# Two norms of a two-block transformer placed inside down projections, and queries and keys placed ahead of the other stream's

## The reference, cut to what matters

```python
def second_block(x, c, ctx, ...):
    for i in range(DEPTH):                       # 2 layers: pooling, attention
        a_l = modulate(rms_norm_2(h_lat, norm_g[i, 0]), sh1, sc1)
        a_c = modulate(rms_norm_2(h_ctx, norm_g[i, 0]), csh1, csc1)
        # layer 0: y = pool_mix(a, pool_w, pool_scale), for each stream
        # layer 1: y_l = attn_mix(a_c, a_l, ...): queries of a_l, keys and values of both
        h_lat = h_lat + g1 * y_l
        m_l = modulate(rms_norm_2(h_lat, norm_g[i, 1]), sh2, sc2)
        h_lat = h_lat + g2 * sq_relu_mlp(m_l, mlp_w1[i], mlp_w2[i])
        # layer 0: the same for h_ctx
    return rms_norm_2(h_lat, final_g)

def pool_mix(h, w, scale):      # p: window means of 2, 4, 8, 16 rows, less the row itself
    return einsum("blgc,gcd->blgd", p, w) * scale
```

## Time and profile before

| | us |
|---|---|
| median of 3 runs | 1587.86 (1587.66 to 1589.6) |
| the profiled execution | 1588.41 |
| its span, first to last instruction | 1585.9 |
| busy: PE, DVE, ACT | 1490.0, 1113.0, 760.0 |
| mean granted clock | 0.979 |

### The profile page before, as it was taken

How to read it: one execution, slowest core, us unless ns; L and a number is a source line. 1 busy time by engine, 2 the same in 40 slices (tenths; PEclk the granted TensorE clock), 3 DMA queues, 4 the chain that set the end, 5 groups by cost and what they waited for, 6 DMA issues and landing times.

```text
span 1585.9 us, 21196 instructions
## 1 busy us (share of the span) xinstructions
PE 1490.0 (94%) x8517; PEld 1202.0 (76%) x8517; DVE 1113.0 (70%) x1682; ACT 760.0 (48%) x1184; POOL 0.2 (0%) x4
## 2 busy tenths in 40 slices
PE   5999899999999799999999999899999998899997
PEld 3767778888787568888778878688787776778786
DVE  3566758998769868998676555867767685465656
ACT  3334544444544445344465544555545534455543
POOL 0000000000000000000000000000000000000000
PEclk9999999999999899999999999899999999999999
DMA  9993158888565757776647555486674740245452
GB/s 361 343 320 136 54 186 292 293 286 304 206 239 183 243 186 260 266 245 239 213 151 274 186 186 186 161 302 233 248 255 146 269 140 27 79 133 178 172 189 86
DMA packets 167913, 335.22 MB, mean 211 GB/s; under 512 B 8192, under 2 KB 109192, under 8 KB 167816
## 3 DMA queue, kind: packets, MB, share of 16 engines
q1 hardware_dynamic: 140992, 235.09, 43.8%
q10 hardware_dynamic: 26824, 98.79, 16.8%
HBM read 332.81 MB, written 1.05 MB: 211 GB/s over the span
## 4 chain that ended last, share of the span: by engine, by line
PE 59%; DVE 25%; ACT 8%; DMA 4%; issue 4%; ACTq 0%; SPq 0%; DVEq 0%
PE ps L1860 11%; PE ps L1861 11%; PE ps L1862 11%; PE ps L1929 11%; DVE wlo L1138 9%; PE ps L1930 5%; ACT whi L659 4%; DVE hbuf L1160 3%; DMA ring<-in_ada_w_dram 3%; ACT hbuf L679 2%; PE ps L1791 1%; DVE res L1226 1%; DVE work L1224 1%; PE ps L2024 1%; PE ps L2101 1%
## 5 line engine op out<-in xcount | busy, mean ns | idle before, releaser
L1138 DVE TENSOR_TENSOR wlo<-wraw,whi 128x1024 fp32r<-128x1024 f32 (+1 forms) x420 | 493.2, 1216 | 202.9 <-ACT whi L659 202.3
L659 ACT ACTIVATE whi<-wraw 128x1024 fp32r<-128x1024 f32 (+1 forms) x420 | 418.3, 1044 | 227.0 <-PE ps L1862 139.1
L1929 PE MATMUL ps<-hT,whi 128*128 128x512 f32 x1472 | 519.4, 398 | 2.7 <-DVE hT L1281 2.7
L1930 PE MATMUL ps<-hT,wlo 128*128 128x256 f32 x1472 | 411.1, 279 | 0.0
L1929 PEld LDWEIGHTS ps<-hT,whi 128*128 128x128 f32 x1472 | 276.5, 188 | 74.0 <-DVE hT L1281 4.3
L1930 PEld LDWEIGHTS ps<-hT,wlo 128*128 128x128 f32 x1472 | 277.7, 189 | 0.0
L1860 PE MATMUL ps<-whi,act_hi 128*128 128x512 f32 x560 | 219.6, 392 | 9.0 <-DVE wlo L1138 9.0
L1862 PE MATMUL ps<-whi,act_lo 128*128 128x512 f32 x560 | 218.0, 389 | 0.0
L1861 PE MATMUL ps<-wlo,act_hi 128*128 128x512 f32 x560 | 218.0, 389 | 0.0
L1860 PE MATMUL ps<-whi,hT 128*128 128x512 f32 (+2 forms) x416 | 161.6, 388 | 4.6 <-DVE hT L1281 3.9
L1861 PE MATMUL ps<-wlo,hT 128*128 128x512 f32 (+2 forms) x416 | 158.7, 382 | 0.0
(11 more groups left out here) (230 smaller groups left out, 1398.8 us busy)
## 6 DMA issues: line engine op xcount, KB each, us to landing
wraw<-in_mlp_w_dram SPq DMA_DIRECT2D x96, 1024.0 KB, 5.3
ring<-in_ada_w_dram ACTq DMA_DIRECT2D x64, 1024.0 KB, 7.0
work<-in_ada_w_dram ACTq DMA_DIRECT2D x28, 1024.0 KB, 7.6
wraw<-in_ffn_w_gate_dram SPq DMA_DIRECT2D x22, 1024.0 KB, 5.5
wraw<-in_ffn_w_up_dram SPq DMA_DIRECT2D x22, 1024.0 KB, 6.8
wraw<-in_ffn_w_down_dram SPq DMA_DIRECT2D x22, 1024.0 KB, 5.0
wraw<-in_diff_w_in_dram SPq DMA_DIRECT2D x12, 1024.0 KB, 5.2
wraw<-in_attn_w_qkv_dram SPq DMA_DIRECT2D x12, 1024.0 KB, 5.0
```

Of the source, the lines that this page charges most:

```text
L659: nc.scalar.activation(whi[:, u % 2, part], raw_view(u)[:, part], ACT.Copy).then_inc(hi_ready, 1)
L1138: nc.vector.tensor_tensor(wlo[:, u % 2, part], raw_view(u)[:, part], whi[:, u % 2, part].bitcast(F32), ALU.subtract).then_inc(lo_ready, 1)
L1929: mm(ps[:, bank, :], whi[:, u % 2, c0:c0 + P], hT[:, :, k, :], start=(k == 0), stop=False, skip_group_check=True)
L1930: ins = mm(ps[:, bank, 0:S], wlo[:, u % 2, c0:c0 + P], hT_hi[:, k, :], start=False, stop=(k == KT - 1), skip_group_check=True)
```

## The change

The pooling norm of the context (norm 6) moves into down20: ACT squares, DVE scales and TensorE multiplies by the pooling matrices between down20's units, in three PSUM banks that down20 does not use. Pool1 follows down20's last unit; it waits for the residual bank by bank (`bank_emptied`), and its gate is spread behind it, into banks 0 and 1. The latent norm of the attention layer moves into down21 in the same way, as norm 8. The order of the row segments becomes q3, kvl, kvc: the context's norm, now norm 9, is squared and scaled beside q3, transposed and modulated beside kvl, and placed in `hT` column pair by column pair as kvl's units end. The head norms follow the new order, the context's last.

Vectors 18 and 19 are summed by DVE beside up20 and down20, vectors 20 to 23 beside up21 and down21 (before: 20 and 21 alone, 16 adds; now 32 adds in each pair of segments). Their turn in the order changes, the columns of the attention layer move from the attention to q3, and the counts of idle products change. The DMAs of the pooling matrices and scale for the context go out in ACT's iteration 6 of down20. The diff, cut to its core, first what all engines share:

```diff
-        IDLE_NORM = {1: 7, 2: 6, 4: 2, 8: 6, 9: 2, 10: 5}
+        IDLE_NORM = {1: 7, 2: 6, 4: 2, 10: 5}
-        IDLE_HEADS = {1: 5, 3: 46}
+        IDLE_HEADS = {1: 5, 3: 20}
+        IDLE_POOL = 9
-        seg("kvc", "row", [QKV[:, :, 1024:2048]], 4)
         seg("q3", "row", [QKV[:, :, 0:1024]], 4)
         seg("kvl", "row", [QKV[:, :, 1024:2048]], 4)
+        seg("kvc", "row", [QKV[:, :, 1024:2048]], 4)
...
-                     (("up1", "down1"), (15, 16), 1, 27), (("up21", "down21"), (20, 21), 2, 26)]
+        def slots(first, last, many):
+            return [first + n * (last - first) // many for n in range(many)]
+        LATE = ("up20", "down20", "up21", "down21")
...
+                     (("up1", "down1"), (15, 16), slots(1, 27, 32)), (LATE, (18, 19), slots(1, 16, 20) + slots(18, 28, 12)),
+                     (LATE, (20, 21, 22, 23), slots(33, 48, 20) + slots(50, 60, 12))]
...
-                 (1, 3, 0), (0, 3, 0), (0, 3, 1)]
+                 (0, 3, 0), (1, 3, 0), (0, 3, 1)]
+        BESIDE_DOWN = (6, 8)
+        BESIDE_ROWS = 9
+        T_BANKS[6] = T_BANKS[8] = (0, 1, 3, 0)
+        T_BANKS[BESIDE_ROWS] = (0, 1, 3, ADA_BANK)
+        POOL_GATE_BANKS = (0, 1)
```

On ACT:

```diff
+            def norm_beside_down(i):
+                if i == 2:
+                    root_table()
+                if i in (4, 5):
+                    norm_squares((i - 4,))
+                if i == 7:
+                    norm_scale()
+                if i == 10:
+                    norm_columns((1,))
+                if i == 13:
+                    norm_columns((3,))
+            def second_pool(i):
+                if i == 6:
+                    act.wait_ge(lo_ready, 2 * (by_name["down20"]["base"] + 6))
+                    pool_rows(1)
+                norm_beside_down(i)
+            def other_rows(i):
+                if i == 1:
+                    norm_squares()
+                if i == 3:
+                    norm_scale()
+            def other_columns(i):
+                if i == 1:
+                    norm_modulate(1)
+                    norm_modulate(3)
+                if i == 2:
+                    norm_place(1)
```

On DVE:

```diff
+            def norm_beside_down(i):
+                if i == 6:
+                    norm_rows()
+                if i == 10:
+                    norm_columns((0,))
+                if i == 14:
+                    norm_columns((1,))
...
+                else:
+                    held_split("down20")
+                    pool_gate(1, POOL_GATE_BANKS)
                 residual(s_)
                 norm()
...
+            def other_rows(i):
+                if i == 2:
+                    norm_rows()
+                if i == 3:
+                    columns(3, 1)
+            def other_columns(i):
+                if i == 1:
+                    norm_modulate()
+                if i == 2:
+                    norm_place(0)
+                    norm_place(1)
+                if i == 3:
+                    norm_place(2)
+                else:
+                    heads3(1, (i,))
+            row_segment("q3", heads=other_rows)
+            panel_rows(q3, 0, 1024)
+            held_split("q3")
+            row_segment("kvl", heads=other_columns)
+            panel_rows(kvl, 0, 1024)
+            norm_place(3)
+            held_split("kvl")
+            heads3(1, (3,))
+            row_segment("kvc", heads=lambda i: heads3(2, range(i, min(i + 1, 3))))
+            panel_rows(kvc, 0, 1024)
             heads3(2, (3,))
+            heads3(0, range(4))
...
-            attention(3, beside=lambda i: columns(3, 1) if i == 2 else None)
+            attention(3)
```

On TensorE:

```diff
+            def norm_beside_down(i):
+                if i == 9:
+                    norm((0, 1, 2))
+                if i == 12:
+                    norm((3,))
...
-                else:
-                    vector_units(18, 2, 4)
-                    vector_units(19, 0, 2)
-                gate()
-                norm()
+                    gate()
+                    norm()
...
-                if strm == 0:
-                    vector_units(18, 0, 2)
-                else:
-                    vector_units(19, 2, 4)
+                if strm == 1:
+                    gate(POOL_GATE_BANKS)
+                idle_products(T_BANKS[6][2], IDLE_POOL)
                 gate()
                 norm()
...
+                down_segment(f"down2{strm}", beside=norm_beside_down)
-            vector_units(22, 0, 4)
-            norm()
+            row_segment("q3", beside=lambda i: columns(3, 1, 24) if i == 2 else None)
+            row_segment("kvl", beside=lambda i: norm() if i == 1 else None)
             row_segment("kvc")
-            vector_units(23, 0, 2)
-            norm()
-            row_segment("q3")
-            row_segment("kvl")
-            vector_units(23, 2, 4)
             gate()
             idle_products(IDLE_BANK, IDLE_HEADS[3])
-            columns(3, 1, 24)
             pe.wait_ge(sem("heads3"), 1)
```

More of the change, by code:

```diff
@@ L435, in build @@
         PANEL_SEGS = ["in0_2", "in0_0", "in0_1", "out0", "down0", "in1_0", "in1_1", "in1_2", "out1", "down1",
-                      "pool0", "down20", "pool1", "down21", "kvc", "q3", "kvl", "out3", "down3"]
+                      "pool0", "down20", "pool1", "down21", "q3", "kvl", "kvc", "out3", "down3"]
         panel_end = [by_name[n_]["base"] + by_name[n_]["count"] for n_ in PANEL_SEGS]
@@ L698, in stream @@
                         ring_fill(fill_to)
+                    if beside is not None:
+                        beside(i)
                     if s_["kind"] == "down" and i == s_["count"] - 4:
@@ L746, in norm_rows @@
                 junk = full.rearrange("p (q a) n -> p q (a n)", q=4)
-                for t in range(TT):
+                for t in tiles:
                     for h in range(2):
@@ L1294, in norm_columns @@
                     link(modulated(5))
-                    link(nc.vector.tensor_copy(hT_hi[:, 4:6, :], full[:, 4:6, :]))
+                    link(nc.vector.tensor_copy(hT_hi[:, 4:6, :], cols[:, 4:6, :]))
                     low(slice(4, 6))
@@ L1298, in norm_columns, with pool_gate @@
                     low(slice(6, 8))
+            def pool_gate(s_, banks):
+                dve.wait_ge(sem("pool_landed"), 32 * (s_ + 1))
+                for h in range(2):
+                    dve.wait_ge(gate_psum, 2 * (4 + 2 * s_) + h + 1)
+                    nc.vector.tensor_tensor(gate_b[:, 512 * h:512 * h + 512], ps[:, banks[h], :], wk(2048 + 512 * h, 512), ALU.mult).then_inc(sem("pool_gate"), 1)
             def norm():
@@ L1702, in _ @@
                 split_unit(by_name[f"pool{s_}"]["base"] + 2)
-                stream(f"up2{s_}", beside=lambda i: vector_out(19) if s_ == 1 and i == 1 else columns(3, 0) if s_ == 1 and i == 3 else None)
-                stream(f"down2{s_}", hold_last=True)
+                stream(f"up2{s_}", beside=lambda i: columns(3, 0) if s_ == 1 and i == 5 else None)
+                stream(f"down2{s_}", hold_last=True, beside=norm_beside_down)
                 residual(s_)
-            norm()
             held_split("down21")
-            row_segment("kvc", heads=lambda i: vector_out(22) if i == 0 else None)
-            panel_rows(kvc, 0, 1024)
-            norm()
-            held_split("kvc")
             acos = [const("ax_cos").rearrange("p (t a b d) -> p t a b d", t=TT, a=1, b=2)[:, t] for t in range(TT)]
@@ L1974, in down_segment, with norm @@
                         beside(i)
-            def norm():
-                n = norm_no[0]
-                norm_no[0] += 1
-                strm = NORMS[n][0]
+            def norm(blocks=(0, 1, 2, 3)):
+                if 0 in blocks:
+                    norm_no[0] += 1
+                n = norm_no[0] - 1
                 if n in PLAIN:
@@ L1983, in norm @@
                 mats = wk(0, 4 * TT * POOL_BAND).rearrange("p (g j n) -> p g j n", g=4, j=TT)
-                idle_products(IDLE_BANK, IDLE_NORM.get(n, 0))
-                for b in range(4):
+                if 0 in blocks:
+                    idle_products(IDLE_BANK, IDLE_NORM.get(n, 0))
+                for b in blocks:
+                    if b == 3 and n in BESIDE_DOWN:
+                        pe.wait_ge(sem("hT_ready"), len(HT_STEPS) * n + 2)
+                    if b == 3 and n == BESIDE_ROWS:
+                        bank7_wait()
                     if b % 2 == 0:
@@ L2014, in gate @@
                 idle_products(IDLE_BANK, IDLE_GATE.get(e, 0))
-                for t in range(TT):
-                    emptied(n, t)
+                if banks is D_BANKS:
+                    for t in range(TT):
+                        emptied(n, t)
                 pe.wait_ge(mod_rows, VECTOR_AT.index(6 * l + 3 * f + 2) + 1)
```

185 lines of the change are left out of this document (115 added, 70 removed).

## The result

The changed kernel takes 1573.26 us (median of 14 runs, 1566.31 to 1582.84) against 1587.76 for the kernel before (14 runs, 1581.81 to 1592.88) on the same chip: ratio 0.9908, 95% interval 0.9890 to 0.9926, 14.6 us less. The forecast was 1580.3, 7.6 less, with a range from 1574 to 1587. The profiled execution took 1575.97 us (span 1574.2), 12.4 less than the one before.

What follows compares the result with a forecast made beforehand. TensorE's products plus the stretches waiting for a VectorE chain were taken to bound the kernel; −1.5 +0.5 +5.0 −8.3 +1.5 +2.6 −7.4 = −7.6 gave 1580.8 profiled, 1580.3 median. Range 1574 to 1587.

Steps and rivals of the forecast that it cites:

- Adds in the up stages: Up20 and up21: one DVE add fits a unit's ACT and DVE round, two exceed it; +0.5 and +1.5 us.
- Down20: Down20: pooling products and vector 19's summed rows lengthen PE, which has no free time there; +5.0 us.
- down21: Down21: the first stream's norm adds 16 transposes, and one more vector is summed; +2.6 us.
- The fourth rival: Down20: PE waits behind unit 9 for the pooling matrices, some 4 us, 1584.3 in all; chance 0.05.
- The first hole: Down20's last product to up21's first: 22.0 us instead of 30.3, the pool's gate coming late; −8.3 us.
- the 0.3 for a slower gate: First hole: 0.3 us added for a slower gate to the 6.1 us from the second residual's end to up21.
- Pool0's hole: Pool0's hole: vector 18's DMA wait goes, gate and transposes avoid the half clock's delay; −1.5 us.
- The second hole: Down21's last product to the mark that releases the turns: 96.2 us instead of 103.6; −7.4 us.
- U: Time of down21's last product, 1210.7 in the profile before; the second hole's forecast times count from it.
- The first rival: Second hole: DVE becomes its bound altogether, leaving 1.4 of the 7.4 us, 1586.3 in all; chance 0.13.
- The second rival: Ten double units of up20 and up21: second add not covered, 14 us in place of 2, 1592.3; chance 0.07.
- The third rival: Before up21 and in kvc: half clock costs 2.8 us each instead of 0.3 and 1.2, 1584.4; chance 0.09.

Runs made afterwards that it cites:

- the singles: Changed kernel with one add a unit in up20 and up21 (15 each), 17 in place of 12 in the down stage behind: up20 92.19 us, ratio 0.9942.
- the two runs with the same idle products: Changed kernel with kvc's split ahead of q3's rotation and idle products 14, 23 and four behind each gate: 0.9911; with two copies also moved to ACT: 0.9889.
- the run with the split first: Changed kernel with q3's second gain and rotation behind the split of kvc's third unit instead of ahead: second hole 95.05 us, ratio 0.9910.
- the second comparison: Changed kernel unaltered, measured once more against the kernel before on the same chip: 1577.59 us, ratio 0.9928.
- the last run: Changed kernel with kvc's split ahead of q3's rotation, more idle products, and second-tile copies of kvl and kvc moved from DVE to ACT: 1570.34 us, 0.9889.

## Why the prediction was right, and where it was wrong

**The step that failed** is "Adds in the up stages": "the round binds, and DVE's excess is paid in full", with +0.5 in up20 and +1.5 in up21. Measured are -1.0 in up20, and in up21 with down21 +1.8, which is 0.8 under the +2.6 of the norm and the summed vector. Together that is 3.8 us from the forecast, more than the whole error of the sum in the profiles (-7.6 against -10.7). Three things went wrong in it. The round ends up20, though it does not bind in every unit (the 5.74 that it read is a mean of units at PE's own 5.55 and of units at 5.81), but DVE's second add is not over it: the singles gained nothing there. In up21 of the changed kernel no unit takes 5.81 at all: columns and summing products stand between its units (two of them took 5.90 and 6.31), so the round has time and no excess is paid. And the step looked at DVE's half of the round alone. ACT's half held what the diff took out of it, the batches of four transfers, 1.41 us each: without them the kernel before becomes 1.1 and 1.2 us shorter, with four the changed one becomes 1.5 or more longer in up20. The prediction counted the pooling DMAs "behind ring fills" and never priced the ring fills themselves.

**Down20** (+5.0) and **down21** (+2.6 in its units; its whole is 93.7 and 92.9 where the shifting boundary falls in its first unit) lengthened as worked out, by products. PE's pauses at the first three units, up to 1.2 us each, are those of the kernel before; behind them it has none. The fourth rival is out.

**The first hole**: -8.8 against -8.3, and -9.3 against the profile that the forecast was worked out from. The order and the late gate came as written; the end of the second residual came 0.7 earlier because the first one could start 0.4 sooner and the gate's multiplication waited 0.51 instead of 0.8, and the 0.3 for a slower gate was not needed.

**Pool0's hole**: -0.5 against -1.5, less than two profiles of one kernel differ by. In the first profile of the changed kernel the gate ran in 2.44 as forecast, but the transposes started 0.5 later than forecast and took 3.65 instead of the earlier trace rows's 3.36; in the second they started in time and took 3.06. The price rested on the half clock of one profile: the second profile of before has nearly the same wait (2.19) and a gate at 2.50, with its window at 0.87:

```profile
805.40:807.60 2.20, 0.02 (x3) 0.00 (x0) 2.13 (x4) 1.67 (x6) 0.00 (x0) 1.00 0.89 294
...
808.60:811.10 2.50, 2.35 (x12) 0.89 (x9) 1.78 (x8) 1.65 (x5) 0.00 (x0) 0.87 0.17 60
```

The Trainium skill, "TensorE: Matmul & The Clock Gate", Part 1, calls the number of products that run slow at a kernel's start "run-variable". In these traces it varies within a kernel too: this gate took 3.81 and 2.50 in two profiles of the kernel before, and the two runs with the same idle products had their transposes at 1.00 and 0.63.

**The second hole**: -7.2 against -7.4, with PE's pause at 5.02 (5.2 forecast). Behind it the clock fell to 0.50 (window of the changed kernel below), as forecast. That kvc ended at U+83.3, forecast 83.1, is luck in part: its third unit started 0.7 before the forecast (U+69.6) and took 8.1 us instead of 5.4, so the slow clock cost PE 2.7 where the sum had 1.7.

```profile
1276.00:1278.00 2.00, 1.69 (x4) 1.43 (x5) 2.00 (x4) 0.00 (x0) 0.00 (x0) 0.50 0.00 0
```

The first rival (DVE as the bound of that whole stretch) did not cost what it would have, but it names what binds there: the split moved ahead freed PE and hardly the turns, and two copies off DVE gave 3.4. The second rival, the slower one, had the right edge and the wrong place for this change: two adds lie on the edge, three beyond it.

The third rival's condition came true in both places, and its time did not. The transposes before up21 ran at half clock, but the 6.1 us that the forecast took over from the kernel before held that already (timeline of PE, before):

```profile
1023.39 3.65 PE L1998 MATMUL ps<-cst,work 128*128 128x128 f32 x16 [0.26 <-ACT work L762]
```

And kvc's 2.7 us can have reached the turns only in small part, since 7.9 us less on PE there gave 1.4 in the run with the split first.

**The range** ended 0.7 above the result because the bounds of the up stages went from 0 in up20 and +0.5 in up21 upward; none allowed them to become shorter. By the second comparison (0.9928, so 1576.3 us) the time lies inside the range; of the 3.9 us that the profiles do not place the cause stays open.

## What to carry to other kernels

Where a stage ends by a round of two engines, list everything that either engine does in a unit, DMA issues too, and look for changes of that list on both before pricing one. A batch of DMA issues was cheaper here one by one beside ACT's other work than all at once. An engine without pauses sets the end whatever the others gain: here work had to leave DVE, not only stand earlier on PE.

## What the runs showed of the hardware

One ring transfer issued by ACT in a unit made its next copy no later (the single ones of the changed kernel's up21 leave no such pause), two 0.37 us (0.42 and 0.51 in two other profiles), four 1.41, and four with a quarter of the bytes 1.41 too.

The granted clock fell to half behind a gate with no pause over 0.3 us ahead of it (0.61 and 0.63 in the last run), and stayed at 1.00 in another run with the same order of work. The idle products did not secure it.

A unit of 16 wide and 16 narrow products takes 5.55 us in some stretches and 5.65 in others, at the same granted clock of 1.00, and the pace mostly changes where a wait or other products stand between the units. In up21 of the changed kernel (timeline of PE, first products of the third and fourth units, then of the eighth and ninth) units start 5.54 and 5.66 apart:

```profile
1032.61 0.39 PE L2078 MATMUL ps<-hT,whi 128*128 128x512 f32 x1
...
1038.15 0.39 PE L2078 MATMUL ps<-hT,whi 128*128 128x512 f32 x1
...
1060.99 0.40 PE L2078 MATMUL ps<-hT,whi 128*128 128x512 f32 x1
...
1066.65 0.40 PE L2078 MATMUL ps<-hT,whi 128*128 128x512 f32 x1
```

Up20 ran at 5.55 in one profile of the kernel before and at 5.65 in the other, up to the units that the round ends; where the round ends the stage this changes nothing (93.01 and 93.10). What selects the pace was not tried.
